# Sample rows of the FFN down products in four column places, a gate with its k tiles outermost, and later steps of the samples' softmax

## What is computed

```python
def merge_and_ffn(x, o_att, c, ga, gb, w_att, conv_ln_w, conv_ln_b, w_conv_out, w_out,
                  norm_ffn_w, w_gate_up, w_down):
    a = o_att.reshape(*o_att.shape[:-2], D_ATT_OUT) @ w_att
    cb = jax.nn.silu(layer_norm(c, conv_ln_w, conv_ln_b)) @ w_conv_out
    h = jax.nn.sigmoid(ga) * a + jax.nn.sigmoid(gb) * cb
    x = x + h @ w_out
    gu = rms_norm(x, norm_ffn_w) @ w_gate_up
    g, up = gu[..., :D_FF], gu[..., D_FF:]
    return x + (jax.nn.silu(g) * up) @ w_down
...
q, k, v, u, ga, gb = branch_inputs(x, ...)      # z = rms_norm(x) @ w_in, cut into its parts
outs, lses = window_attn_...(q, k, v, window, dil)   # three groups of 4 heads; samples also read a cache
o_att = combine_groups(outs, lses)
c = causal_dwconv(u_ext, conv_w, conv_b)
```

## Time and profile before

| | |
|---|---|
| median of 3 runs | 1767.64 us (1766.23 to 1770.68) |
| the profiled execution's own time | 1770.01 us |
| its span, first to last instruction | 1768.1 us |
| PE busy | 1709.0 us, 97% of the span |
| PEld / DVE / ACT / POOL busy | 1588.8 / 1045.7 / 458.2 / 70.7 us |
| mean granted TensorE clock | 0.994 of full speed |

### The profile page before, as it was taken

The page is one execution under the profiler, slowest core; times in us unless marked ns, Lnnn a source line. Parts: engine busy times, 40 slices in busy tenths (PEclk is TensorE's granted clock), DMA queues, the critical chain, the costliest instruction groups (busy, mean ns, idle before and its releaser), DMA issues.

```text
span 1768.1 us, 25426 instructions
## 1 busy us (share of the span) xinstructions
PE 1709.0 (97%) x10488; PEld 1588.8 (90%) x10488; DVE 1045.7 (59%) x1471; ACT 458.2 (26%) x900; POOL 70.7 (4%) x127
## 2 busy tenths in 40 slices
PE   5999999999999989999999999999999999999999
PEld 5899999999988879889777899989989899899897
DVE  5698898797999767585654424243342442433435
ACT  5111132323353455512222321111112111111110
POOL 0000000000000002120300000000000000000000
PEclk9999999999999999999999999999999999999999
DMA  6111153334333438984860022222222222122232
GB/s 201 48 41 59 59 172 121 96 120 144 115 109 134 141 116 263 298 284 156 292 214 1 36 96 69 87 96 96 96 88 91 96 96 96 63 92 96 95 115 98
DMA packets 155870, 211.55 MB, mean 120 GB/s; under 512 B 8378, under 2 KB 126490, under 8 KB 154987
## 3 DMA queue, kind: packets, MB, share of 16 engines
q1 hardware_dynamic: 145451, 134.01, 24.6%
q0 software_dynamic: 10320, 76.16, 11.3%
HBM read 180.04 MB, written 74.80 MB: 144 GB/s over the span
## 4 chain that ended last, share of the span: by engine, by line
PE 81%; DVE 10%; DMA 3%; DVEq 3%; issue 2%; ACT 1%; ACTq 0%; SPq 0%
PE ps L758 19%; PE ps L759 19%; PE ps L760 19%; PE ps L1213 5%; PE ps L1211 5%; PE ps L1212 5%; DVE conv L1574 3%; PE ps L1131 1%; PE ps L1133 1%; PE ps L1132 1%; PE ps L846 1%; DMA qb<-scr_q 1%; DMA sga<-scr_z 1%; PE ps L959 1%; DVEq L1630 1%
## 5 line engine op out<-in xcount | busy, mean ns | idle before, releaser
L758 PE MATMUL ps<-xhi,whi 128*128 128x352 f32 x1200 | 404.1, 337 | 1.6 <-DVE xlo L1549 1.6
L760 PE MATMUL ps<-xhi,wlo 128*128 128x352 f32 x1200 | 387.1, 323 | 0.0
L759 PE MATMUL ps<-xlo,whi 128*128 128x352 f32 x1200 | 386.5, 322 | 0.0
L758 PE MATMUL ps<-nhi,whi 128*128 128x352 f32 x1056 | 340.8, 323 | 0.8 <-DVE nlo L1937 0.8
L759 PE MATMUL ps<-nlo,whi 128*128 128x352 f32 x1056 | 338.6, 321 | 0.0
L760 PE MATMUL ps<-nhi,wlo 128*128 128x352 f32 x1056 | 338.3, 320 | 0.0
L1574 DVE SCALAR_TENSOR_TENSOR conv<-u,vec,conv 128x1024 f32<-128x1024 f32 x240 | 308.3, 1285 | 25.7 <-issue 11.2
L1530 DVE TENSOR_TENSOR wlo<-raw,whi 128x1024 fp32r<-128x1024 f32 x126 | 153.6, 1220 | 246.9 <-ACT whi L1301 238.6
L758 PEld LDWEIGHTS ps<-xhi,whi 128*128 128x128 f32 x1200 | 227.0, 189 | 11.7 <-issue 5.5
L759 PEld LDWEIGHTS ps<-xlo,whi 128*128 128x128 f32 x1200 | 227.3, 189 | 4.4
L760 PEld LDWEIGHTS ps<-xhi,wlo 128*128 128x128 f32 x1200 | 226.7, 189 | 0.0
(11 more groups left out here) (230 smaller groups left out, 1938.9 us busy)
## 6 DMA issues: line engine op xcount, KB each, us to landing
kv_sample<-cache_kv_w POOLq DMA_DIRECT2D x32, 1022.0 KB, 6.3
raw<-w_in SPq DMA_DIRECT2D x50, 512.0 KB, 4.7
raw<-w_gate_up SPq DMA_DIRECT2D x44, 512.0 KB, 3.9
scr_z<-zt SPq DMA_DIRECT2D x34, 528.0 KB, 3.2
qb<-scr_q POOLq DMA_DIRECT2D x24, 512.0 KB, 6.1
raw<-w_down SPq DMA_DIRECT2D x22, 512.0 KB, 4.0
kc<-cache_kv_w POOLq DMA_DIRECT2D x16, 512.0 KB, 6.7
kv_sample<-cache_kv_w POOLq DMA_DIRECT2D x8, 1016.0 KB, 6.4
```

The source lines that it names most:

```text
L758: pe_mm(out, wh, rhs_hi, start=first, stop=False)
L759: pe_mm(out, wh, rhs_lo, start=False, stop=False)
L760: return pe_mm(out, wl, rhs_hi, start=False, stop=last)
```

## The change

It has three parts.

**FFN down products of the samples.** The samples' activations are kept whole (`acs`, plain fp32, 32 columns), and the weights are taken from `raw`, before their split. Each product of 32 weight columns with 512 fp32 columns fills one quarter of the array's columns. The four products of a round (two halves by two k tiles) go to four column places, PSUM partitions 0, 32, 64 and 96, none accumulates on another, and DVE adds all four into `x1s`. They run ahead of the prompt's units, so the units are numbered anew (`down_unit`): 0 and 1 are the samples, 2 to 17 the prompt. The next load into `raw` now also waits for them. `y_sample` is written in one piece, ahead of the prompt's last stores.

**Last gate.** Slots 45 to 47 become one block with the k tiles outermost, in banks 3 to 5 (`last_gate`). After each k tile it signals `s_xk`, and `conv_hi` may overwrite that tile of `xhi`. The tanh of the three chunks comes after `conv_hi` on ACT.

**Steps of the samples' softmax.** `new_scores` moves from slot 60 to 61, `row_logits` from 60 to 61, the exponent and `row_norm` from 61 to 62, `row_probs` and the copy to `ptr` from 62 to 64, and TURN_SLOT from 64 to 65.

```diff
-TURN_SLOT = 64
+TURN_SLOT = 65
...
-    achl = [at(f"achl{i}", [P, 2, 2 * NS], F32R, S5 + 8 * T * 4 + i * 4 * NS * 4) for i in range(2)]
+    acs = [at(f"acs{i}", [P, 2, NS], F32, S5 + 8 * T * 4 + i * 4 * NS * 4) for i in range(2)]
...
+    s_xk, XK0 = s_tr, 2 * (KT + 1)
...
-                eng.wait_ge(s_dn, DNG * i + NT * (t + 1))
+                eng.wait_ge(s_dn, DNG * i + down_unit(t, KT - 1) + 1)
...
+    def down_unit(half, t):
+
+        return 2 + KT * half + t
...
         for n in range(FFN0 + 2, NJOBS):
+            kind, i, half = FFN_JOBS[n - 2 - FFN0]
+            if kind == "down":
+                sp.wait_ge(s_dn, DNG * i + half + 1)
             ffn_load(n)
...
+        sp.wait_ge(s_add, DNG * (NIT - 1) + 2)
+        sp.dma_start(a["y_sample"].rearrange("b s d -> (b s) d"), x1s[:, :]).then_inc(s_yst, 16)
         for half in range(2):
-            cc = slice(half * 512, half * 512 + 512)
-            for t in range(NT):
-                sp.wait_ge(s_add, DNG * (NIT - 1) + NT * half + t + 1)
-                dst = a["y_prompt"][0, t * P:(t + 1) * P, cc] if t < KT else a["y_sample"].rearrange("b s d -> (b s) d")[:, cc]
-                sp.dma_start(dst, x1_half(t, half)).then_inc(s_yst, 16)
-        sp.wait_ge(s_yst, 16 * DNG)
+            for t in range(KT):
+                sp.wait_ge(s_add, DNG * (NIT - 1) + down_unit(half, t) + 1)
+                sp.dma_start(a["y_prompt"][0, t * P:(t + 1) * P, half * 512:half * 512 + 512], x1_half(t, half)).then_inc(s_yst, 16)
+        sp.wait_ge(s_yst, 16 * (DNG - 1))
...
+        def last_gate():
+
+            pe.wait_ge(s_lo, CO0)
+            pe.wait_ge(s_Oe, NB)
+            for k in range(KT):
+                for c in range(NCH):
+                    mm = split_products(z(1, c), wk(1, k), k, xhi[:, k, cols(c)], xlo[:, k, cols(c)], k == 0, k == KT - 1)
+                    if k == KT - 1:
+                        mm.then_inc(s_g, 1)
+                    elif c == NCH - 1:
+                        mm.then_inc(s_xk, 1)
+
         def first_conv_out():
 
             pe.wait_ge(s_lo, CO0 + 1)
-            pe.wait_ge(s_zta, NCH * 2 * KT)
+            pe.wait_ge(s_zta, NCH * (2 * KT - 1))
             for k in range(KT):
...
-            if q == CO_SLOT:
+            if q == CO_SLOT - NCH:
+                last_gate()
+            elif q == CO_SLOT:
                 first_conv_out()
-            elif q >= CO_SLOT + NCH or q < CO_SLOT:
+            elif q >= CO_SLOT + NCH or q < CO_SLOT - NCH:
                 dense(q)
...
-            if q == DEC_SLOT + 1:
+            if q == DEC_SLOT + 2:
                 new_scores()
-            if q == DEC_SLOT + 3:
+            if q == DEC_SLOT + 5:
                 row_probs()
...
+        def down_free(i, d):
+
+            if d >= RING:
+                pe.wait_ge(s_add, DNG * i + d - RING + 1)
+            elif i + 1 < NIT:
+                pe.wait_ge((s_sil, s_gt)[d // NCH], 2 * NCH * (i + 1) + NCH + d % NCH + 1)
+            else:
+                pe.wait_ge(s_add, DNG * i - RING + d + 1)
+
+        def down_samples(i):
+
+            for half in range(2):
+                n = down_job(i) + half
+                pe.wait_ge(s_raw[n % 2], 16 * (n // 2) + 16)
+                down_free(i, half)
+            for half in range(2):
+                for k in range(2):
+                    p = 2 * NS * half + NS * k
+                    mm = nc.tensor.matmul(ps[p:p + NS, half, :], acs[i % 2][:, k, :], raw[(down_job(i) + half) % 2][:, k * 512:k * 512 + 512],
+                                          start=True, stop=True, skip_group_check=True)
+                mm.then_inc(s_dn, 1)
+
         def down(i, half):
 
             pe.wait_ge(s_lo, down_job(i) + half + 1)
-            for t in range(NT):
-                n, d = rows_of(t), NT * half + t
-                if d >= RING:
-                    pe.wait_ge(s_add, DNG * i + d - RING + 1)
-                elif i + 1 < NIT:
-                    pe.wait_ge((s_sil, s_gt)[d // NCH], 2 * NCH * (i + 1) + NCH + d % NCH + 1)
-                else:
-                    pe.wait_ge(s_add, DNG * i - RING + d + 1)
-                dst, tok = ps[0:n, d % RING, :], slice(t * P, t * P + n)
-                if t == KT:
-                    for k in range(2):
-                        cc = slice(k * 512, k * 512 + 512)
-                        nc.tensor.matmul(ps[0:2 * NS, d % RING, :], achl[i % 2][:, k, :], whi[half][:, cc], start=k == 0, stop=False, skip_group_check=True)
-                        mm = nc.tensor.matmul(dst, achl[i % 2][:, k, 0:NS], wlo[half][:, cc], start=False, stop=k == 1, skip_group_check=True)
-                    mm.then_inc(s_dn, 1)
-                    continue
+            for t in range(KT):
+                d = down_unit(half, t)
+                down_free(i, d)
+                dst, tok = ps[:, d % RING, :], slice(t * P, t * P + P)
                 for k in range(2):
...
+            down_samples(i)
             for half in range(2):
                 down(i, half)
...
-            act.activation(zt[m % 2][:, cols(c)], z(0, c), ACT.Tanh, scale=0.5).then_inc(s_zta, 1)
+            act.activation(zt[m % 2][:, cols(c)], z(jj == 2 * KT - 1, c), ACT.Tanh, scale=0.5).then_inc(s_zta, 1)
...
         def conv_hi():
-            act.wait_ge(s_g, CO_SLOT)
             act.drain()
             for k in range(KT):
+                if k < KT - 1:
+                    act.wait_ge(s_xk, XK0 + k + 1)
+                else:
+                    act.wait_ge(s_g, CO_SLOT)
                 act.copy(shi[:, k, :], conv[:, k, :]).then_inc(s_shi, 1)
...
-            if q < CO_SLOT:
+            if q < CO_SLOT - NCH:
                 gate(q)
...
-            if q == CO_SLOT - 1:
+            if q == CO_SLOT - NCH:
                 conv_hi()
+                for x in range(NCH):
+                    gate(q + x)
-            if q == DEC_SLOT + 2:
+            if q == DEC_SLOT + 3:
                 act.wait_ge(s_prow, 1)
                 act.activation(prow[:, :, :], prow[:, :, :], ACT.Exp, bias=sst[:, 1:2], scale=SCALE, accum_out=sst[:, 2:3]).then_inc(s_pexp0, 1)
-            if q == DEC_SLOT + 3:
+            if q == DEC_SLOT + 5:
...
-                        act.copy(achl[i % 2][:, t, 0:NS], sil[t][:, SEQ:T]).then_inc(s_ahi2, 1)
+                        act.copy(acs[i % 2][:, t, :], sil[t][:, SEQ:T]).then_inc(s_ahi2, 1)
...
-            if q == CO_SLOT - 1:
+            if q == CO_SLOT - NCH:
                 for k in range(KT):
                     conv_lo(k)
-            if q == DEC_SLOT + 1:
+            if q == DEC_SLOT + 2:
                 row_logits()
-            if q == DEC_SLOT + 2:
+            if q == DEC_SLOT + 3:
...
-                        V.tensor_tensor(aclo[i % 2][:, t, 2 * CH:SEQ], sil[t][:, 2 * CH:SEQ], achi[i % 2][:, t, 2 * CH:SEQ].bitcast(F32), ALU.subtract)
-                        V.tensor_tensor(achl[i % 2][:, t, NS:2 * NS], sil[t][:, SEQ:T], achl[i % 2][:, t, 0:NS].bitcast(F32), ALU.subtract).then_inc(s_alo2, 1)
+                        V.tensor_tensor(aclo[i % 2][:, t, 2 * CH:SEQ], sil[t][:, 2 * CH:SEQ], achi[i % 2][:, t, 2 * CH:SEQ].bitcast(F32), ALU.subtract).then_inc(s_alo2, 1)
...
-            for t in range(NT):
-                n, d = rows_of(t), NT * half + t
+            if half == 0:
+                for x in range(2):
+                    xs = x1s[:, x * 512:x * 512 + 512]
+                    dve.wait_ge(s_dn, DNG * i + x + 1)
+                    V.tensor_tensor(xs, xs, ps[2 * NS * x:2 * NS * x + NS, x, :], ALU.add)
+                    dve.drain()
+                    V.tensor_tensor(xs, xs, ps[2 * NS * x + NS:2 * NS * x + 2 * NS, x, :], ALU.add).then_inc(s_add, 1)
+            for t in range(KT):
+                d = down_unit(half, t)
                 dve.wait_ge(s_dn, DNG * i + d + 1)
-                last = V.tensor_tensor(x1_half(t, half), x1_half(t, half), ps[0:n, d % RING, :], ALU.add)
-                if t == KT:
-                    dve.drain()
-                    last = V.tensor_tensor(x1_half(t, half), x1_half(t, half), ps[NS:2 * NS, d % RING, :], ALU.add)
-                last.then_inc(s_add, 1)
+                V.tensor_tensor(x1_half(t, half), x1_half(t, half), ps[:, d % RING, :], ALU.add).then_inc(s_add, 1)
```

## The result

The changed kernel takes **1752.37 us**, median of 4 runs (1750.79 to 1753.75), beside 1767.05 us (median of 4) for the kernel before on the same chip: a ratio of 0.9915, 95% interval 0.9902 to 0.9927. That is 15.0 us faster by the ratio (12.9 to 17.3), where 14.4 were forecast, against the median of 3 runs, 1767.64. The profiled execution took 1750.79 us, its span 1749.0 us.

What follows compares the result with a forecast made beforehand. PE was taken to bound the kernel, four fifths of the span being its own work and the FFN PE alone. Gains of 6.9 + 0.4 + 1.3 + 5.8 = 14.4 us off 1767.64 gave 1753.2 us, range 1748 to 1761.

Steps and rivals of the forecast that it cites:

- The sum: Whole kernel: gains of 6.9 + 0.4 + 1.3 + 5.8 = 14.4 us, giving 1753.2 us.
- Part 1, 6.9 us: FFN down products of the samples: 20.0 us removed, 13.1 us added in 11 rounds of 1.19 us.
- passage: PE's switch to plain fp32 and back around the samples' products, 0.31 us a round.
- the staircase: Rival for the samples' FFN products: records start in program order, 2.51 us a round, a loss of 7.6 us; chance 0.04.
- What else part 1 moves: FFN down: PE's new waits, loads into `raw` and DVE's four earlier adds cost nothing; adds end about 6.5 us after its start.
- The end, 0.4 us: Kernel's tail: one last add and a store, 3.1 us instead of 3.5; gain 0.4 us, between 0 and 0.8.
- Part 2, 1.3 us: Last gate: the 3.08 us wait at first conv-out goes, but `sgc` holds DVE's gate; gain 1.3 us, bounds 0 and 3.1.
- Part 3, 5.8 us: Samples' softmax steps, slots 60 to 65: 2.1 of 6.36 us of waits remain; gain 5.8 us, bounds 2.4 and 8.1.
- The walk through DVE's rows: Slots 60 to 65 in DVE's new order: division ends at 810.05, `row_probs` waits 0.6 us, turns end at 817.0.
- the removed half clock: Half clock behind the long wait at `row_probs`, 807.30 to 810.00, should not come; it had cost about 1.5 us.
- What was costed at nothing: Later turns bring `woraw` 4 us later against PE; DVE idles between gates there, so no cost.

Runs made afterwards that it cites:

- repeat of before: The kernel before, run again without an edit for a second profile: ratio 0.9999 to the kernel before.
- part 3 alone: The kernel before with only the samples' softmax steps and turns moved to their later slots: 1761.15 us, 0.9968.
- the probabilities one slot earlier: The changed kernel with `row_probs` and the copy to `ptr` at slot 63 and not 64: 1756.63 us, 0.9942.
- repeat of after: The changed kernel, run again without an edit for a second profile: ratio 0.9915 to the kernel before.
- one place: The changed kernel with all four sample products of a round in the first column place, a half's two k tiles accumulating: 1780.37 us, 1.007.
- part 1 alone: The kernel before with only the samples' FFN down products in four column places: 1761.24 us, 0.9968.
- row loads later: The changed kernel with SP's samples' row loads issued in slot 50, not 44, behind the `sgc` loads: 1749.25 us, 0.99.
- two places: The changed kernel with a round's sample products in two column places, one for each half, in two banks: 1761.68 us, 0.9965.
- both moves: The changed kernel with SP's row loads in slot 50 and DVE's merge of the attention groups at slot 57, not 55: 1749.34 us, 0.9906.
- later merge: The changed kernel with DVE's merge of the prompt's three attention groups at slot 57, not 55: 1749.86 us, 0.9896.

## Why the prediction was right

- **The sum.** 14.4 us forecast, 15.0 by the ratio (12.9 to 17.3); 1753.2 us forecast, 1752.37 measured. The mechanisms held in all three parts. That the sum is so close is in part luck: part 1 gave a little less than its term, and parts 2 and 3 differ from theirs by up to 1.8 us, to either side, with the profile that one compares with.
- **Part 1, 6.9 us.** The round's cost of 1.19 us, read from the cache products of the earlier trace rows, was measured at 1.18; its streaming 0.86 for 0.88 and its passage 0.32 for 0.31. A whole round of the FFN became only 0.60 us shorter, though, for the 0.63 of the sum. Where the 0.03 us are lost is not shown. That the two banks would not matter was a choice that no row covered, and the runs with one and two places bear it out. *Program order:* the Trainium skill (TensorE: Matmul & The Clock Gate, Part 3, What overlaps and what doesn't) has matmuls start in program order. Four records start within 0.05 us here, the second records of each product behind them. So this trace, in which a product is read as two records, disagrees with the staircase that the rule would make, as the earlier trace rows did.
- **What else part 1 moves.** No wait of PE for an add or a raw tile. DVE's first add comes 3.4 us after the down's start (3.5 forecast), and the four end at 6.3 (6.5):

```profile
1078.82 0.67 DVE L2030 TENSOR_TENSOR x1s<-x1s,ps 32x512 f32<-32x512 f32 x1
...
1081.03 0.69 DVE L2032 TENSOR_TENSOR x1s<-x1s,ps 32x512 f32<-32x512 f32 x1
```

- **The end, 0.4 us.** The last add starts at 1745.85 and the span ends 3.15 us later, 3.1 forecast; before, it was 3.5.

```profile
1745.85 0.69 DVE L2036 TENSOR_TENSOR x<-x,ps 128x512 f32<-128x512 f32 x1 [0.69 <-PE ps L1245]
```

- **Part 2, 1.3 us.** The mechanism held: `sgc` is issued 19.9 us after slot 45 as before (20.0), the gate follows 4.3 us later, and stands 24.1 us after slot 45 where it stood 25.9: 1.8 us gained. The forecast's own 742.02 and 4.5 us give 746.5 for the landing, not the 746.6 that it used, and so 1.4 us. The size is uncertain in both directions. Slot 45 to 51 takes 25.5 to 27.2 us in the seven profiles that have the new gate and the row loads ahead of `sgc`, against 27.6 in the first profile of before. Against the repeat of before, 29.0, the gain is 2.5 to 3.1 us in the two profiles of the changed kernel, since the removed wait had brought half clock with it there. The forecast took the wait of 3.08 us at its length alone.
- **Part 3, 5.8 us.** 6.4 us against the first profile, 4.9 against the repeat, and 5.7 (3.7 to 7.6) by the times of part 3 alone. The walk through DVE's rows held to 0.1 us: the division was to end 23.0 us after the start of slot 60 (810.05 less 787.09) and does (806.42 less 783.41). It gave a wait of 1.5 us at slot 61, which was 1.19 where the clock did not hide it, and one of 0.6 ahead of `row_probs`, of which 0.18 came, since slot 64 ended 0.3 to 0.5 us later than in the walk. `row_probs` itself costs 0.63 us and not the 1.2 that the walk took: that was read from a stretch at half clock (0.50 in the earlier trace rows), while the walk forecast full clock there. So the walk ended 0.6 us late, and the gain was 0.6 us too small. The other way, the 1.5 us that the removed half clock was to give behind the long wait were there in the first profile of before only. In the other three profiles that have the old steps the half clock came at slot 61, ahead of that wait, which was 2.4 us instead of 3.9. So the term was too low for the profile that it was read from (6.4) and too high for the others (4.9), and its closeness to the measured 5.7 is luck. The margin at `row_probs` is thin, as the run with the probabilities one slot earlier shows. PE at `row_probs` and slot 65 in the repeat of after:

```profile
807.03 0.87 PE L1034 MATMUL ps<-ident,prow 128*128 128x128 f32 x6 [0.18 <-DVE prow L1778]
807.66 0.41 PE L766 MATMUL ps<-shi,whi 128*128 128x352 f32 x1
```

- **What was costed at nothing.** The later `woraw`: ACT takes it up at 823.74, with slot 66 at 812.7, and no wait of PE follows.

The profiled execution of the changed kernel lies 4.8 us below the 1755.6 that the sum gives for the like of the first one of before. That is the 2.8 us ahead of slot 45 and the 1.9 us of clock between slot 66 and the FFN. The first is not the change's doing. The prediction put such a stretch down to chance and gave it no term; that it is chance is not shown.

## What to carry to other kernels

Small products that fill a quarter of the array's columns are worth putting in four column places even at the price of plain fp32: here 4 x 0.86 us of streaming became 0.86, and with the 0.32 us of passage that is 1.18 us where the old form took 1.82 and one place would take 3.75. The price could be read ahead from another line of the same form. Before moving a step to take away a wait, walk through the other engine's rows in their new order up to the next hand-over: the wait is gone only if the consumer stands behind the producer's new end, and one slot too early gave most of it back. A length read from a stretch at half clock must not go into a sum for full clock. A wait of PE may cost more than its length, or less, so waits are best compared over several profiles.

## What the runs showed of the hardware

**Half clock behind some waits and not behind others.** Granted clock 0.50, the lower of the two levels (1.2 GHz), came behind or at the end of the wait of about 3.1 us at the first conv-out in three of the four profiles that have this wait. At slot 60 it came behind 2.52 us in the repeat of before, 2.17 us in the changed kernel and 1.97 us with the probabilities earlier, but not behind 2.19 us with part 1 alone, 1.95 us in the changed kernel's repeat or 2.38 us with the row loads later. At slot 51 a wait of 3.42 us in the changed kernel's repeat passed without it. So the length of a wait alone did not tell whether it would come.

Between slot 66 and the FFN PE waits twice for about 2.1 us in most profiles (for `va` and for DVE's `hl`), and behind both, one or none of these a half-clock stretch follows. All five profiles of kernels that lack a part of the change have two such stretches, both profiles of the changed kernel have one, and its six variants have two (two places; both moves, where one of the two is behind a wait of 1.25 us), one (earlier probabilities; later merge) or none (one place; later row loads). The table by stretch for before, after, and the later row loads:

```profile
820.00:1000.00 180.00, 173.17 (x976) 143.63 (x975) 92.20 (x166) 48.60 (x93) 17.75 (x27) 0.98 0.45 151
```

```profile
820.00:1000.00 180.00, 172.74 (x986) 143.87 (x985) 91.43 (x165) 51.78 (x100) 18.26 (x28) 0.99 0.42 142
```

```profile
820.00:1000.00 180.00, 172.61 (x994) 144.22 (x993) 91.49 (x165) 52.16 (x100) 18.27 (x28) 1.00 0.44 148
```

From slot 66 to the FFN these take 169.2, 167.3 and 165.9 us with two, one and none, so one costs about 1.7 us. No run here moves these stretches on purpose, so what sets their number, and whether the change lowers it, stays open.

**Column places.** A plain fp32 product of 512 columns costs its place 0.86 us whether the other three are empty (one place, 3.75 us a round) or full (four places, 1.18 us), and two places in two banks run side by side (2.04 us).
